# Turning the 16-key strips of the attention probabilities with the whole identity instead of its last 32 columns

## The reference, cut to what matters

```
probs = jax.nn.softmax(jnp.where(mask, logits, NEG), axis=-1)        # rows: queries, columns: keys
return jnp.einsum('bhqk,bkhd->bqhd', probs.astype(v.dtype), v)       # causal: no key after the query
```

## Time and profile before

| what | value |
| --- | --- |
| median of three runs | 3218.52 us (3216.46 to 3221.98) |
| the profiled execution, its own time | 3217.61 us |
| its span, first to last instruction | 3215.8 us |
| TensorE busy | 2992.7 us, 93% of the span |
| VectorE busy | 1683.6 us, 52% |
| ScalarE busy | 995.5 us, 31% |
| GpSimd busy | 570.3 us, 18% |
| mean granted TensorE clock | 0.984 of full speed |

### The profile page before, as it was taken

The page is one execution under the profiler, slowest core; times in us unless marked ns, Lnnn a source line. Parts: engine busy times, 40 slices in busy tenths (PEclk is TensorE's granted clock), DMA queues, the critical chain, the costliest instruction groups (busy, mean ns, idle before and its releaser), DMA issues. The chain is left out here.

```text
span 3215.8 us, 41507 instructions
## 1 busy us (share of the span) xinstructions
PE 2992.7 (93%) x14982; PEld 1739.1 (54%) x14982; DVE 1683.6 (52%) x4531; ACT 995.5 (31%) x2765; POOL 570.3 (18%) x994
## 2 busy tenths in 40 slices
PE   5899999999899999989998999999988999999999
PEld 4445666655456666644453456665544556665443
DVE  4226887766667534421132378777667764434122
ACT  1223333333344433310012333333344443333000
POOL 1001222111111123310000012221111211333000
PEclk8999999999999999999999999999999999999999
DMA  5101111101000012042120011101010000210421
GB/s 205 48 27 34 41 42 31 39 30 48 16 21 16 21 31 95 16 148 78 53 84 27 7 44 40 40 30 42 25 52 14 16 16 30 91 30 24 132 70 50
DMA packets 91011, 153.15 MB, mean 48 GB/s; under 512 B 12657, under 2 KB 68225, under 8 KB 88761
## 3 DMA queue, kind: packets, MB, share of 16 engines
q1 hardware_dynamic: 90808, 150.50, 14.3%
HBM read 120.36 MB, written 32.21 MB: 47 GB/s over the span
## 5 line engine op out<-in xcount | busy, mean ns | idle before, releaser
L988 PE MATMUL ps_s<-xT,w_ring 128*128 128x348 f32 (+2 forms) x3616 | 1139.2, 469 | 4.5 <-DVE gate L1406 2.8
L988 PEld LDWEIGHTS ps_s<-xT,w_ring 128*128 128x128 f32 x3616 | 676.8, 192 | 393.1 <-issue 97.8
L1568 POOL TENSOR_SCALAR arena<-arena,small 128x256 f32<-128x256 f32 (+9 forms) x576 | 363.3, 642 | 1539.5 <-DVE small L1481 1538.3
L1223 ACT ACTIVATE arena<-arena,small 128x256 f32<-128x256 f32 (+9 forms) x576 | 380.2, 660 | 168.4 <-DVE small L1469 167.6
L1234 ACT ACTIVATE arena<-ps_t 128x512 f32<-128x512 f32 (+4 forms) x700 | 282.0, 435 | 360.3 <-PE ps_t L1060 328.4
L1264 DVE MAX8 small<-score 128x8 f32<-128x1040 f32 (+6 forms) x448 | 376.4, 840 | 10.5
L1266 DVE MATCH_REPLACE8 score<-small,score 128x1040 f32<-128x1040 f32 (+6 forms) x448 | 370.0, 826 | 0.0
L1032 PE MATMUL ps_s<-feat 64*128 64x256 f32 (+12 forms) x1888 | 308.3, 428 | 28.7 <-DVE small L1469 24.4
L1072 PE MATMUL ps_o<-arena 128*64 128x256 f32 (+3 forms) x3200 | 288.7, 319 | 21.0 <-ACT cT L1157 14.4
L1060 PE MATMUL ps_t<-ident,arena 128*128 128x128 f32 (+2 forms) x2048 | 301.1, 275 | 6.1 <-DVE arena L1433 3.3
L1087 PE MATMUL ps_s<-arena,feat 128*128 128x512 f32 x640 | 286.0, 600 | 10.4 <-DMA arena<-in_w_out 10.4
(11 more groups left out here) (146 smaller groups left out, 2489.0 us busy)
## 6 DMA issues: line engine op xcount, KB each, us to landing
w_ring<-in_w_feat SPq DMA_DIRECT2D x78, 512.0 KB, 3.6
mixed<-mixg SPq DMA_DIRECT2D x128, 128.0 KB, 1.7
feat<-mixed SPq DMA_DIRECT2D x16, 1024.0 KB, 6.6
resid<-score SPq DMA_DIRECT2D x16, 512.0 KB, 3.2
score<-resid SPq DMA_DIRECT2D x16, 512.0 KB, 7.4
arena<-in_w_out SPq DMA_DIRECT2D x4, 1536.0 KB, 8.0
cT<-falls SPq DMA_DIRECT2D x8, 520.0 KB, 4.9
feat<-falls SPq DMA_DIRECT2D x8, 520.0 KB, 5.3
```

The costliest lines, as they stand in the source:

```text
L988: mm = pe.matmul(ps_s[:, bank, 0:w], w_ring[:, wt % 2, k, :], xT[:, k, c0:c0 + w], start=(k == 0), stop=(k == KT - 1))
L1223: nc.scalar.activation(p, p, ACT.Exp, scale=-1.0, bias=nm[:, e:e + 1], accum_out=psums[0:M, st % 4, e:e + 1]).then_inc(S["exp_done"], 1)
L1568: nc.gpsimd.tensor_scalar(p, p, rinv[0:M, st % 4, e:e + 1], 1.0, ALU.mult, ALU.mult).then_inc(S["nrm_done"], 1)
```

## The change

The branch for the strips goes: each strip is turned by the same transpose as the full tiles, with all 128 columns of the identity moving. Its output is then 16 keys by 128 queries and fills its 128 columns of the bank. The copy takes the last 32 of these instead of the first 32. For all other tiles M equals `it["M"]`, so their slice stays what it was.

```
-                src = src[:, :, first:first + k, 0:M]
+                src = src[:, :, first:first + k, it["M"] - M:it["M"]]
```

```
                             k0, w = key_cols(it["br"], i, kb)
-                            m = asks(it["br"], i, kb)
-                            if m < M:
-                                mm = pe.matmul(ps_t[0:w, tg % 2, c * BLK:c * BLK + m], p_row(it, h, k0, w),
-                                               ident[:, BLK - m:BLK], start=True, stop=True)
-                                continue
                             mm = pe.transpose(ps_t[0:w, tg % 2, c * BLK:c * BLK + M], p_row(it, h, k0, w),
                                               ident[0:M, 0:M])
```

## The result

The changed kernel takes 3223.61 us (median of 20 runs, 3221.68 to 3225.41), the kernel before 3218.62 us in 20 runs beside them. The ratio is 1.0015, with a 95% interval of 1.0008 to 1.0022: slower by 5.0 us, 2.6 to 7.1. That is less than the 0.2% set as the bound, and above zero.

A forecast was written before the change was run, and what follows sets the result against it. The prediction took TensorE, busy 93% of the span, as the bound; +10.9 behind waits, -6.0 in block 1 and -0.2 in C gave +4.7 us. It forecast 3222.5 us, range 3213 to 3231.

The forecast's parts named there:

- The bound: TensorE, busy for 93% of the span: a change there is paid in full unless it falls into its waits.
- Strips at once: 83 groups starting straight behind earlier work: 59 come out even, two in C's last pair give -0.2 us in all.
- Strips behind a wait: 109 groups starting after a wait for a bank: 0.32 us to the scores instead of 0.22, +10.9 us in all.
- Block 1: 24 mixed groups (full, strip, full, strip): 0.53 us instead of 0.78, so -0.25 us each, -6.0 in all.
- Sum: All strip groups together: +10.9 - 6.0 - 0.2 = +4.7 us.
- First rival: Every step from transpose to strip stays at 0.20 us instead of 0.11: +15 us, 3233; 2%.
- Second: Rival: the 0.10 us behind the waits is absorbed, as ACT's copy chain sets the next wait's end: 3212; 11%.
- Third: Rival: transposes between waits bring the lower clock more often in B and C: +20 us more, 3243, 2%; weaker 3229, 5%.
- The clock: Stretches at 1.2 GHz anywhere in the kernel, added or removed by shifted starts: +-3 us in either direction, beside the sum.
- forecast case: The summed terms hold, with clock +-3 us and 0.02 us either way in 109 waits: 3217 to 3229; 72%.

The follow-up runs named there:

- e5: The changed kernel with each of the 384 strips turned twice, the second result overwriting the first: 3260.98 us, ratio 1.0128 to the kernel before.
- e1: The kernel before with only block 1's strips (24 mixed groups) turned by transposes, all others keeping the short matmul: 3217.17 us, ratio 0.9997.
- e8: The kernel before with 128 weight columns instead of 16 in the strip's short matmul, still 32 moving columns: 3257.81 us, ratio 1.0121.
- e9: e1 with its block 1 strips turned twice: 3219.24 us, ratio 1.0000 to the kernel before.
- e10: The same kernel as e1 run once more, beside e9 on one chip: 3217.23 us, ratio 0.9995 to the kernel before.
- e2: The kernel before with the strips of blocks 2 to 8 turned by transposes, block 1 keeping its short matmuls: 3232.60 us, ratio 1.0047.

## Why the prediction was right

Its forecast was 3222.5, no measurable change with a lean to slower; 3223.6 came out.

- *The bound.* TensorE's time was paid nearly in full: of 10.2 us more at the strips 1.4 came back at later waits, where the prediction had said that nothing gives it back. In e5, with the strips doubled, it was 3.8 more.
- *Strips at once.* Even, as said: within 4 ns in blocks 2 to 4 of A and B, by the starts followed through both traces. The last pair of C in each layer gave 0.096 at the strips, and 0.10 more one pass later.
- *Strips behind a wait.* +0.092 to +0.099 us for each of the 109 groups, +0.10 forecast. The reason, that the change of form had been hidden in the wait, has its counterpart in the idle time, unchanged at 43.9 us.
- *Block 1.* -0.257 us, -0.25 forecast. The credit is there in both the whole change and e1.
- *Sum.* +4.0 at the strips, +4.7 forecast; the difference is the rounding to 0.10 and 0.25. That the median then rose by 5.0, so near to 4.7, is in part luck: with what came back the strips are worth +2.6, and the lower clock filled the gap.
- *First rival* (the form stays changed): a strip follows a full tile at 0.11 us, and e8 shows on what the form hangs. Out. *Second* (absorbed): out by the idle time and by e5, but for the 1.4 us above. *Third* (the clock by transposes): e9 turns block 1's strips twice as often as e10, and has the higher clock. Against it, at this size.
- *The clock.* This was the term that was mis-sized. I gave it +-3 us as chance in either direction. In e1 and e2 it is worth up to 5.8 and 5.2 us by the estimate above, to the slow side in every run. In the changed kernel itself it is smaller: +2.2 us in the profiled execution, and at most 1.6 by a mean clock of 0.9835 against 0.984. With the strips' +2.6 that makes some 4.2 to 4.8 of the median's 5.0, inside its interval.
- *The range.* The upper end of the forecast case's own range, 3229, doesn't follow from its terms: 3 us of clock and 0.02 us in 109 waits are 5.2 us either way, which ends at 3227.7.

## What to carry to other kernels

Price a short matmul between others by the distance of starts, and look for the step in and out of its form: with 16 weight columns each cost 0.09 us here, three times the pass itself. Then ask for each place whether a wait already covers that step, because there its removal is worth nothing and a longer instruction costs its length, unless a wait for something else stands behind it. And where three groups share two banks, a free place in a full group was worth 31 us, while the form of the instruction was worth 5: remove the wait first.

## What the runs showed of the hardware that was not expected

- A two-pass matmul of 32 moving columns takes 0.03 us for a pass with 16 weight columns and 0.11 with 128, the same as a transpose of 128 columns, though the load of the weights is shown as running beside the matmul. With 32 moving columns it is the number of weight columns that sets the pace here.
- The share of the time at 1.2 GHz follows small shifts of the work in a reproducible way: 0.984 in 22 of 22 runs of before on one chip and 18 of 21 on another, 0.982 or 0.983 in all 11 runs of e1 on the one and all 11 of e10 on the other, which differ from it by 0.26 us in each of 24 places. In this kernel a gain of 6 us all but vanished beside it: 0.7 us of 6.2 was left in the median, and the lower clock accounts for at most 5.8 by the estimate above.
